# Adds moved to GpSimd, a channel norm over summed blocks, and one instruction block instead of two

## The chip, the cores and the metric

One core of one Trainium2 chip runs the kernel. The metric is the device time of one execution in microseconds (us). Five engines work from queues of their own: TensorE (PE; PEld is its weight load), VectorE (DVE), ScalarE (ACT), GpSimd (POOL) and SyncE (SP, which issues most of the DMAs). They wait for each other at semaphores.

## The reference

Two layers over a sequence of 1024 tokens of width 1024, all in fp32. What the change touches:

```python
# first block, its end
p_ssm = y_ssm @ w_branch_ssm;  p_att = y_att @ w_branch_att
merged = sigmoid(g_ssm) * p_ssm + sigmoid(g_att) * p_att
x = x + rmsnorm(merged @ w_out) * post_g
# second block
h = rms_norm(x);  proj = h @ w_in                        # conv (a, gate), q, k, v, two gates
y = causal_depthwise_conv(a * sigmoid(gate), width 31) + b   # 512 channels
conv = silu(layer_norm(y over the 512 channels))
attn = rms_norm(diff_attention(rms_norm(q), rms_norm(k), v))
merged = gate0 * (conv @ w_conv_out) + gate1 * (attn @ w_attn_out)
x = x + merged @ w_out
h2 = rms_norm(x)
x = x + mixture_of_experts(h2)                           # 32 experts, top 2 in one of 4 groups
```

## The kernel before

The kernel is a row of stages, each a set of programs for the five engines. Every large product keeps fp32 accuracy with three fp32r matmuls: high x high, high x low and low x high parts. ScalarE writes the high part (a rounded copy), VectorE the low part (the raw value less the high part).

`phase_dense` is the common loop. It takes a list of jobs, each a product with 512 output columns for the eight tiles of 128, whose results fill the eight PSUM banks. A step n is one k of one job: 24 matmuls of 512 columns. For each step ScalarE makes the high parts of the activations (L898) and of the weights (L880), VectorE the low parts (L945, L936), two steps ahead of TensorE at most. Behind the last k of a job the banks are evicted: by ScalarE (`act`, L922), or by VectorE as a multiply (`mul_T`, L972) or as a multiply and an add (`muladd_T`, L982 and L986, a pair for each bank, the second behind the first). TensorE starts a bank of the next job when its eviction is done. The last job walks the banks in the order 0, 2, 4, 6, 1, 3, 5, 7 (`HALVES`). Hooks let other work ride along in an engine's order: `aside(n)` on VectorE behind the low parts of step n, `beside(n)` on ScalarE behind the high parts, `middle[n]` on TensorE ahead of step n, `fill` on GpSimd, `fetch` on SyncE.

The stages in order: constants and the first norm; dense `xbc`; `phase_ssd`; then in one block the dense phase `bs`, the forgetting attention, dense `za` (its jobs 4 and 5, with eight steps each, are `muladd_T`), `phase_out_norm` and dense `q2` (2 x sigmoid and product, k, q, v). The block ends. `Chip.sem` registers a clear of each semaphore on GpSimd (L143), run when its stack is closed; `Chip.stage` closes it behind the block and then sets a barrier over all engines (L155). The next block holds `phase_diff_attention`, dense `gb2` and `phase_out_route`, and a third, with its own set of semaphores, the experts.

`gb2` has four gate jobs of eight steps (0 to 31), then two `mul_T` jobs with the attention output and two `muladd_T` jobs with the convolution's output, of four steps each (32 to 47). VectorE runs the convolution as taps (L741: source times a tap plus the accumulator, both in SBUF), two or three per step, in q2 and in gb2 up to step 31. `ChannelNorm` follows as hooks, counted from MEAN = 32: TensorE sums the four blocks of 128 channels with a matrix of ones ahead of step 32 (L2196, eight products of fp32 with 512 columns), ScalarE takes the mean (L2217), VectorE centres the blocks at steps 33 and 34 (L2239), ScalarE squares them at 34 and 35 (L2222), TensorE sums the squares ahead of step 36, VectorE adds eps at 37 (L2243), ScalarE takes the root at 38 (L2225), VectorE the reciprocal at 38 (L2247) and the products at 39 (L2251), ScalarE the Silus at 39 (L2230). Their result is the input of jobs 6 and 7, steps 40 on, which wait for it. The same hooks carry the split of the output weights (L3342 and L3355, one every second step).

The router ends with VectorE writing the slots of the tokens (L2461 to L2465) and GpSimd gathering the rows of the first two experts (L2509). The experts stage (`expert_programs`) loads each expert's three matrices of 2 MB, splits them (L2892 on ScalarE, L2957 on VectorE), turns the gathered rows (L2817), splits those (L2908, L2972), multiplies (L2808), and scatters with an add (L2782). A matrix's raw buffer is reloaded by SyncE as soon as its low parts are made. Gathers for later experts are L2765.

## Time and profile before

| | us |
|---|---|
| median of 3 runs (3044.0 to 3046.78) | 3046.55 |
| the profiled execution, its own time | 3043.43 |
| its span, first to last instruction | 3041.6 |
| mean granted TensorE clock | 0.961 |
| q2: last matmul starts / ScalarE's last eviction ends | 1792.53 / 1793.56 |
| gb2: last tap ends / low parts of step 35 end | 2129.98 / 2158.1 |
| gb2: TensorE starts steps 32, 36, 40, 44, 46 | 2143.97, 2174.75, 2206.70, 2230.50, 2249.84 |
| gb2: VectorE's evictions and low parts of step 37 end | 2171.19 |
| the router's first product starts | 2262.09 |
| VectorE writes the last slots | 2402.31 |
| the experts' first product starts / the last scatter is issued | 2421.69 / 3017.84 |

Times of the trace count from the start of the span. Engines overlap, so busy shares don't add up; idle time of an engine matters only where TensorE, or in the experts the transfers, wait for it. A row of a timeline gives the start, the duration (of all instructions merged in it), the engine, the line, and in brackets the idle time ahead of it with what ended that.

### The profile page before, as it was taken

The numbers are of one execution on the slowest core, as the hardware profiler recorded it, in microseconds if no ns is written. First come the engines' busy times: TensorE is split into PE (matmuls) and PEld (weight loads), VectorE is DVE, ScalarE is ACT, GpSimd is POOL, SyncE is SP. The second block draws the span as 40 slices with busy tenths as digits, with TensorE's granted clock in tenths as the row PEclk, the third lists the DMA queues.
The fourth block names the chain that finished last, engine by engine and source line by source line (L and its number), as shares of the span: only waits on it lengthen the run. The fifth ranks groups of instructions, "written<-read, shape, count | busy, mean of one in ns | idle before, by whom it ended". The sixth has DMA issues, their size and how long they took to land. (4 is left out here: it accounts for less than half of the span.)

```text
span 3041.6 us, 36124 instructions
## 1 busy us (share of the span) xinstructions
PE 2792.5 (92%) x13292; PEld 2281.5 (75%) x13302; DVE 1901.3 (63%) x2142; ACT 1440.0 (47%) x2105; POOL 482.1 (16%) x375
## 2 busy tenths in 40 slices
PE   6998999999989989999989987899899599999996
PEld 5787977888867666887878866778678488888874
DVE  3776745444345554435544876799563599888885
ACT  2544435323336655333333445533422277777773
POOL 0001400000006664000000000000000134434331
PEclk9999999999989999999999998999999699999998
DMA  3110011213466663121211100111212499999994
GB/s 93 42 49 15 1 57 42 101 46 104 159 187 132 139 131 77 49 104 42 91 56 51 49 15 1 29 46 46 89 53 116 172 364 384 369 366 368 363 356 150
DMA packets 159435, 387.95 MB, mean 128 GB/s; under 512 B 72769, under 2 KB 72897, under 8 KB 134720
## 3 DMA queue, kind: packets, MB, share of 16 engines
q1 hardware_dynamic: 150080, 369.27, 36.3%
q0 software_dynamic: 9216, 16.81, 2.2%
q8 instruction: 90, 1.47, 0.2%
q14 instruction: 49, 0.40, 0.0%
HBM read 347.93 MB, written 54.85 MB: 132 GB/s over the span
## 5 line engine op out<-in xcount | busy, mean ns | idle before, releaser
L2957 DVE TENSOR_TENSOR ex_w<-ex_raw,ex_w 128x2048 fp32r<-128x2048 f32 x190 | 430.8, 2289 | 77.5 <-ACT ex_w L2892 75.8
L2892 ACT ACTIVATE ex_w<-ex_raw 128x2048 fp32r<-128x2048 f32 x190 | 361.8, 1916 | 143.0 <-DMA ex_raw<-in_w_up_e 62.4
L2808 PE MATMUL ps<-ex_w,ex_xT 128*128 128x512 f32 x1536 | 368.3, 396 | 15.5 <-DVE ex_xT L2972 15.4
L2808 PEld LDWEIGHTS ps<-ex_w,ex_xT 128*128 128x128 f32 x1536 | 287.0, 190 | 82.0 <-issue 13.7
L945 DVE TENSOR_TENSOR bs_t<-arena,bs_t 128x1024 fp32r<-128x1024 f32 x88 | 107.7, 1224 | 270.0 <-ACT bs_t L898 269.9
L898 ACT ACTIVATE bs_t<-arena 128x1024 fp32r<-128x1024 f32 x88 | 93.3, 1061 | 294.6 <-PE ps L841 280.8
L741 DVE SCALAR_TENSOR_TENSOR arena<-arena,small 128x1023 f32<-128x1023 f32 (+9 forms) x168 | 213.5, 1271 | 3.6
L1276 POOL TENSOR_TENSOR fa_pl<-fa_p,fa_ph 128x512 fp32r<-128x512 f32 x192 | 191.9, 1015 | 103.5 <-ACT fa_ph L1397 100.8
L2808 PE MATMUL ps<-ex_w,ex_hT 128*128 128x512 f32 x768 | 182.9, 394 | 1.3 <-issue 1.1
L839 PE MATMUL ps<-bs_t,bs_w 128*128 128x512 f32 x448 | 175.3, 391 | 7.9 <-DVE bs_w L936 4.3
L840 PE MATMUL ps<-bs_t,bs_w 128*128 128x512 f32 x448 | 174.4, 389 | 0.0
L841 PE MATMUL ps<-bs_t,bs_w 128*128 128x512 f32 x448 | 174.3, 389 | 0.0
L839 PE MATMUL ps<-gb_t,gb_w 128*128 128x512 f32 x368 | 147.1, 400 | 20.9 <-DVE arena L972 7.0
L2808 PEld LDWEIGHTS ps<-ex_w,ex_hT 128*128 128x128 f32 x768 | 141.8, 188 | 31.6 <-issue 2.1
L1432 DVE TENSOR_REDUCE small<-ps 128x1 f32<-128x128 f32 (+7 forms) x128 | 96.7, 757 | 106.4 <-PE ps L1298 105.9
L839 PE MATMUL ps<-za_t,za_w 128*128 128x512 f32 x368 | 146.1, 397 | 8.9 <-DVE arena L986 4.1
L945 DVE TENSOR_TENSOR za_t<-arena,za_t 128x1024 fp32r<-128x1024 f32 x48 | 58.8, 1225 | 147.2 <-ACT za_t L898 147.1
L1387 ACT ACTIVATE fa_p<-ps 128x512 f32<-128x512 f32 x192 | 94.0, 490 | 108.6 <-PE ps L1330 66.1
L840 PE MATMUL ps<-gb_t,gb_w 128*128 128x512 f32 x368 | 145.1, 394 | 0.0
L840 PE MATMUL ps<-za_t,za_w 128*128 128x512 f32 x368 | 145.0, 394 | 0.0
L841 PE MATMUL ps<-gb_t,gb_w 128*128 128x512 f32 x368 | 145.0, 394 | 0.0
L841 PE MATMUL ps<-za_t,za_w 128*128 128x512 f32 x368 | 144.9, 394 | 0.0
(415 smaller groups left out, 6589.6 us busy)
## 6 DMA issues: line engine op xcount, KB each, us to landing
ex_raw<-in_w_gate_e SPq DMA_DIRECT2D x64, 1024.0 KB, 13.7
ex_raw<-in_w_up_e SPq DMA_DIRECT2D x64, 1024.0 KB, 13.1
ex_raw<-in_w_down_e SPq DMA_DIRECT2D x64, 1024.0 KB, 14.1
arena<-in_w_in SPq DMA_DIRECT2D x108, 512.0 KB, 3.5
arena<-in_x SPq DMA_DIRECT2D x4, 2048.0 KB, 11.1
arena<-in_w_out SPq DMA_DIRECT2D x16, 512.0 KB, 6.6
arena<-in_w_branch_ssm SPq DMA_DIRECT2D x8, 512.0 KB, 3.6
att_qh<-bs_split SPq DMA_DIRECT2D x2, 2048.0 KB, 8.8
```

What stands on the lines that cost most here:

```text
L741: ins = dve.scalar_tensor_tensor(out=acc[:, b, back:], in0=src[:, b, 0:SEQ - back], scalar=w, in1=acc[:, b, back:], op0=ALU.mult, op1=ALU.add)
L839: nc.tensor.matmul(c.ps[:, t, :], a[0], b[0], start=(k == 0), stop=False)
L840: nc.tensor.matmul(c.ps[:, t, :], a[0], b[1], start=False, stop=False)
L841: mm = nc.tensor.matmul(c.ps[:, t, :], a[1], b[0], start=False, stop=(n == last[j]))
L898: nc.scalar.activation(tp[s][0], jobs[j][0][:, k, :], ACT.Identity).then_inc(t_high, 1)
L945: V.tensor_tensor(tp[s][1], jobs[j][0][:, k, :], tp[s][0].bitcast(F32), ALU.subtract)\
L1276: nc.gpsimd.tensor_tensor(low[x % 4][:, 0:w], prob[x % 3][:, 0:w], f32(high[x % 4][:, 0:w]), ALU.subtract).then_inc(lowered, 1)
L1387: nc.scalar.activation(prob[x % 3][:, 0:w], c.ps[:, S_BANK[x % 3], 0:w], ACT.Exp)\
L1432: V.tensor_reduce(negmax[h % 2][:, t:t + 1], src, AX.X, ALU.max, negate=True)\
L2808: mm = nc.tensor.matmul(out, l, r, start=(k == 0 and n == 0), stop=(k == kc - 1 and n == 2))
L2892: nc.scalar.activation(half_of(part[m][0], h), raw[m][:, h * W // 2: (h + 1) * W // 2], ACT.Identity).then_inc(high[m], 1)
L2957: V.tensor_tensor(half_of(part[m][1], h), raw[m][:, h * W // 2: (h + 1) * W // 2], half_of(as_f32(part[m][0]), h), ALU.subtract)\
```

## The change

- `Chip.stage` sets no barrier behind its block. `Chip.retire` is new: GpSimd waits for some semaphores, closes a set (clears its semaphores) and signals `retired`. Dense `bs` to the experts now stand in one block with three sets: `first` (bs to out_norm), `second` (q2 and differential attention), `alive` (the rest). `first` is retired in q2, `second` in the last job of gb2. Differential attention waits for `retired[0]` and, engine by engine, for what the block's end stood for; the router waits for `retired[1]`.
- The experts' programs follow the router's in the same block. TensorE's first permissions to write the weights (`used`) move from the start of the experts to the router, behind "chosen".
- In `muladd_T` jobs but the last, VectorE only multiplies; GpSimd adds, bank by bank (semaphore `by_pool`). The merged product waits for all eight adds.
- `ChannelNorm`: GpSimd adds the four blocks and the four squared blocks (`on_pool`), TensorE sums one block over its channels. Root and reciprocal move from step 38 to 37, products and Silus from 39 to 38.

```diff
@@ -152,10 +152,20 @@
-        self.nc.all_engine_barrier()
-Dense = namedtuple("Dense", "product by_act by_vec kept w_low steps")
+    def retire(self, block, sems, waits, retired):
+        @block.gpsimd
+        def _(pool):
+            for s, n in waits:
+                pool.wait_ge(s, n)
+            sems.close()
+            pool.sem_inc(retired, 1)
...
@@ -812,6 +822,12 @@
         def _(pool):
+            for j, job in enumerate(jobs[:-1]):
+                if job[2] == "muladd_T":
+                    for t in range(TT):
+                        pool.wait_ge(by_vec, before(j, False) + t + 1)
+                        nc.gpsimd.tensor_tensor(job[3][:, t, :], job[4][:, t, :], job[3][:, t, :], ALU.add)\
+                            .then_inc(by_pool, 1)
         def _(pe):
...
@@ -978,6 +994,8 @@
+                    elif j < len(jobs) - 1:
+                        y = V.tensor_tensor(other[:, t, :], src, other[:, t, :], ALU.mult)
...
@@ -1534,6 +1552,7 @@
+            act.wait_ge(dense.by_pool, TT)
...
@@ -1919,10 +1938,15 @@
         def _(pe):
+            pe.wait_ge(retired, 1)
+            pe.wait_ge(normed, 2 * TT)
             def lay(x):
+                else:
+                    pe.wait_ge(dense.by_act, 3 * TT + x + 1)
...
@@ -1995,6 +2019,8 @@
         def _(act):
+            act.wait_ge(retired, 1)
+            act.wait_ge(dense.product, 5 * TT)
@@ -2032,6 +2058,9 @@
         def _(dve):
+            dve.wait_ge(retired, 1)
+            dve.wait_ge(dense.tapped, taps)
+            dve.wait_ge(lam.params, 16 * 8)
...
+    def on_pool(self, convolved):
+        pool, T = self.nc.gpsimd, self.nc.gpsimd.tensor_tensor
+        total = self.rstd
+        for b in range(1, self.NB):
+            convolved(pool, b)
+            if b > 1:
+                pool.wait_ge(self.by_blocks, b - 1)
+            T(total, total if b > 1 else self.av[:, 0, :], self.av[:, b, :], ALU.add)\
+                .then_inc(self.by_blocks, 1)
+        for b in range(1, self.NB):
+            pool.wait_ge(self.squared, b + 1)
+            if b > 1:
+                pool.wait_ge(self.by_blocks, self.NB + b - 2)
+            T(self.qv[:, 0, :], self.qv[:, 0, :], self.qv[:, b, :], ALU.add).then_inc(self.by_blocks, 1)
     def over_channels(self, src):
-        for b in range(self.NB):
-            for h in range(2):
-                mm = self.nc.tensor.matmul(c.ps[:, h, :], c.ones[:], src[:, b, h * BANK:(h + 1) * BANK],
-                                           start=(b == 0), stop=(b == self.NB - 1))
+        for h in range(2):
+            mm = self.nc.tensor.matmul(c.ps[:, h, :], c.ones[:], src[:, h * BANK:(h + 1) * BANK],
+                                       start=True, stop=True)
     def mean_on_tensor(self, pe, by_act, by_vec):
-        pe.wait_ge(self.convolved, 1)
-        self.over_channels(self.av).then_inc(self.meaned, 1)
+        pe.wait_ge(self.by_blocks, self.NB - 1)
...
+        self.over_channels(self.rstd).then_inc(self.meaned, 1)
     def variance_on_tensor(self, pe, by_act, by_vec):
-        pe.wait_ge(self.squared, self.NB)
-        self.over_channels(self.qv).then_inc(self.spread, 1)
+        pe.wait_ge(self.by_blocks, 2 * self.NB - 2)
+        self.over_channels(self.qv[:, 0, :]).then_inc(self.spread, 1)
     def on_scalar(self, n):
@@ -2220,10 +2264,10 @@
-        elif n == 6:
+        elif n == 5:
-        elif n == 7:
+        elif n == 6:
@@ -2242,10 +2286,9 @@
-        elif n == 6:
-        elif n == 7:
+        elif n == 6:
...
@@ -2382,6 +2425,7 @@
+            dve.wait_ge(retired, 1)
...
@@ -2597,6 +2644,8 @@
+            for used in experts_may:
+                pe.sem_inc(used, 1)
...
@@ -2877,8 +2926,9 @@
-        for m in range(3):
-            pe.sem_inc(used[m], 1)
+        if extra:
+            for m in range(3):
+                pe.sem_inc(used[m], 1)
...
@@ -3021,16 +3071,13 @@
-    return ExpertPrograms(sync, gpsimd, tensor, scalar, vector, half0, half1, stored)
-def phase_experts(c, x_dram, y_dram, experts, raw, loaded, gathered):
-    with ExitStack() as ctx:
-        main = expert_programs(c, ctx, "ex", x_dram, y_dram, experts, raw, loaded, gathered)
-        more = expert_programs(c, ctx, "xe", x_dram, y_dram, experts, expert_raw(c, True), main=main)
-        block = ctx.enter_context(c.nc.Block())
+    return ExpertPrograms(sync, gpsimd, tensor, scalar, vector, half0, half1, stored, used)
+def phase_experts(main, more, within):
+    with nullcontext(within) as (ctx, block):
...
-        with c.stage() as within:
-            differed = phase_diff_attention(c, q_tok, k_tok, lam, v2, o2, 4, 5, within)
+            c.retire(block, first, [(dense3.product, 2 * TT), (dense3.by_vec, TT), (dense3.w_low, 2 * KC + 1),
+                                    (out_normed.kept, 16 * TT)], retired[0])
+            differed = phase_diff_attention(c, q_tok, k_tok, lam, v2, o2, 4, 5, within, retired[0], dense3,
+                                            qk.normed, IN_Q2[-1])
+            ctx, within = alive, (alive, block)
...
@@ -3341,10 +3383,25 @@
+            def sum_blocks(pool, by_vec, kept):
+                def convolved(pool, b):
+                    if b == 3:
+                        pool.wait_ge(channels.convolved, 1)
+                    else:
+                        pool.wait_ge(blocks_done, b)
+                        pool.wait_ge(heads2.placed, TT)
+                channels.on_pool(convolved)
+            blocks_done = c.sem(ctx, "cn_blocks_done")
             def aside_gb2(n, tapped, by_act, by_vec, moved):
...
+                for b in range(3):
+                    if IN_GB2[n] < CW * (b + 1) - IN_Q2[-1] <= IN_GB2[n + 1]:
+                        nc.vector.wait_ge(tapped, IN_GB2[n + 1])
+                        nc.vector.sem_inc(blocks_done, 1)
                 if n == MEAN - 1:
...
+                        fill=sum_blocks,
+            c.retire(block, second, [(dense2.product, 2 * TT), (dense2.w_low, 2 * KC + 1)], retired[1])
+            main = expert_programs(c, ctx, "ex", xn, out[0], experts, raw, loaded, gathered)
+            more = expert_programs(c, ctx, "xe", xn, out[0], experts, expert_raw(c, True), main=main)
-                            within, parts2, dense2)
-            return c
-        phase_experts(c, xn, out[0], experts, raw, loaded, gathered)
+                            within, parts2, dense2, retired[1], main.used)
+            phase_experts(main, more, within)
...
```

## Rows read from the trace of the kernel before

**Rows 1.** The page, busy time of each engine.

```profile
PE 2792.5 (92%) x13292; PEld 2281.5 (75%) x13302; DVE 1901.3 (63%) x2142; ACT 1440.0 (47%) x2105; POOL 482.1 (16%) x375
```

**Rows 2.** Windows: stretch, its length, busy PE, PEld, DVE, ACT, POOL, clock, DMA share, GB/s.

```profile
2230.00:2250.00 20.00, 15.60 (x50) 11.31 (x50) 13.93 (x20) 4.11 (x5) 0.00 (x0) 0.74 0.00 1
2444.00:2990.00 546.00, 536.72 (x2507) 443.11 (x2506) 489.42 (x298) 407.84 (x296) 216.12 (x114) 1.00 1.00 368
```

**Rows 3.** GpSimd's semaphore clears at the two block ends: count, ns, first and last.

```profile
L143 POOLq EVENT_SEMAPHORE_RANGE_CLEAR  x90: 44/44/44, 1793.8 to 1800.4; - x90
...
L143 POOLq EVENT_SEMAPHORE_RANGE_CLEAR  x51: 44/44/44, 2410.0 to 2413.5; - x51
```

**Rows 4.** Timeline, TensorE and ScalarE behind the first of these.

```profile
1800.80 8.54 PE L1927 MATMUL ps<-ident,arena 128*128 128x128 f32 x64 [7.88 <-PEq L155]
...
1801.99 0.69 ACT L2002 ACTIVATE da_k<-ps,small 128x512 fp32r<-128x512 f32 x1 [8.43 <-PE ps L1927]
```

**Rows 5.** Timeline, TensorE around the gated jobs of za and gb2.

```profile
1413.72 0.47 PE L839 MATMUL ps<-za_t,za_w 128*128 128x512 f32 x1 [0.40 <-PE ps L841]
...
1464.31 0.39 PE L855 MATMUL ps<-za_t,za_w 128*128 128x512 f32 x1
...
2230.50 0.47 PE L839 MATMUL ps<-gb_t,gb_w 128*128 128x512 f32 x1 [0.30 <-PE ps L841]
...
2249.84 0.39 PE L853 MATMUL ps<-gb_t,gb_w 128*128 128x512 f32 x1
```

**Rows 6.** Timeline, VectorE's first multiply and last add of gb2's gated job.

```profile
2228.77 0.68 DVE L982 TENSOR_TENSOR arena<-ps,arena 128x512 f32<-128x512 f32 x1
...
2238.78 0.69 DVE L986 TENSOR_TENSOR arena<-arena 128x512 f32<-128x512 f32 x1
```

**Rows 7.** Timeline, TensorE: the two channel sums, the stalls of steps 39 and 40.

```profile
2135.75 7.10 PE L2196 MATMUL ps<-arena,ones 128*128 128x512 f32 x16 [0.30 <-PE ps L841]
...
2166.33 7.10 PE L2196 MATMUL ps<-arena,ones 128*128 128x512 f32 x16 [0.30 <-PE ps L841]
...
2193.97 0.50 PE L839 MATMUL ps<-gb_t,gb_w 128*128 128x512 f32 x1 [2.56 <-DVE gb_w L936]
...
2206.70 0.77 PE L839 MATMUL ps<-gb_t,gb_w 128*128 128x512 f32 x1 [6.99 <-DVE arena L972]
```

**Rows 8.** Timeline, VectorE and ScalarE: last taps, reciprocal, Silus.

```profile
2127.44 2.54 DVE L741 SCALAR_TENSOR_TENSOR arena<-arena,small 128x995 f32<-128x995 f32 x2
...
2184.55 6.55 DVE L2247 RECIPROCAL arena<-arena 128x1024 f32<-128x1024 f32 x1 [1.07 <-ACT arena L2225]
...
2196.42 4.64 ACT L2230 ACTIVATE arena<-arena,small 128x1024 f32<-128x1024 f32 x4
```

**Rows 9.** Timeline, start of the experts: gather's issue, turn of x, first product.

```profile
2402.95 1.22 POOL L2509 DMA_INDIRECT arena<-expert_in,ints  x1 [31.18 <-DVE ints L2461]
...
2414.65 1.94 PE L2817 MATMUL ps<-ident,arena 128*128 128x128 f32 x8 [13.25 <-DVEq L3018]
2421.69 2.93 PE L2808 MATMUL ps<-ex_w,ex_xT 128*128 128x512 f32 x6 [5.10 <-DVE ex_xT L2972]
```

**Rows 10.** Groups by line and shape: GpSimd's subtractions of 384 and 512 columns.

```profile
L1276 POOL TENSOR_TENSOR fa_pl<-fa_p,fa_ph 128x512 fp32r<-128x512 f32 x96 | 122.5, 1293 | 61.9 <-ACT fa_ph L1397 59.6 <-PE ps L1354 1.5
...
L1276 POOL TENSOR_TENSOR fa_pl<-fa_p,fa_ph 128x384 fp32r<-128x384 f32 x32 | 32.3, 1010 | 2.7 <-ACT fa_ph L1397 2.5
```

**Rows 11.** Timeline, a two-operand product of VectorE beside GpSimd's work and alone.

```profile
1164.96 2.26 DVE L1209 TENSOR_TENSOR arena<-arena,fa_rinv 128x1024 f32<-128x1024 f32 x1
...
1163.61 5.99 POOL L1276 TENSOR_TENSOR fa_pl<-fa_p,fa_ph 128x512 fp32r<-128x512 f32 x4 [0.96 <-ACT fa_ph L1397]
...
1190.51 1.21 DVE L1209 TENSOR_TENSOR arena<-arena,fa_rinv 128x1024 f32<-128x1024 f32 x1
```

**Rows 12.** Groups by line: indirect DMAs and VectorE's subtractions in the experts.

```profile
L2765 POOL DMA_INDIRECT arena<-expert_in,ints x30 | 73.9, 2465 | 27.5 <-POOL ints L2761 26.3 <-issue 1.2
...
L2957 DVE TENSOR_TENSOR ex_w<-ex_raw,ex_w 128x2048 fp32r<-128x2048 f32 x190 | 430.8, 2289 | 77.5 <-ACT ex_w L2892 75.8
```

102 lines of the change are left out of this document (49 added, 53 removed).

## The prediction

> **What bounds the kernel now.** I began with the page. TensorE is busy 92% of the span and no other engine over 63% [rows 1], so a microsecond counts only if TensorE loses it, except in the experts: there the DMA share is 1.00 at 368 GB/s over 546 us, TensorE 98% busy [rows 2]. Earlier stages are serial for TensorE; what they give back moves the experts' first transfer, and the end with it, one for one. Then I went along TensorE's timeline for its idle times. Five kinds lie where the change works: the two ends of a block (the clears of semaphores, then the first rows of TensorE and ScalarE behind them [rows 3, 4]); stalls behind VectorE's multiply-add pairs [rows 5, 6]; the two sums over channels [rows 7]; the stalls around the reciprocal [rows 7, 8]; the start of the experts [rows 9]. A matmul of 512 columns starts every 0.227 us at full clock (24 in a step of 5.44 us) and every 0.427 us at half; a step below is one k of a dense phase.
>
> **The profiled execution.** It took 3043.43 us; the median is 3046.55, 3.1 us (0.1%) more. I subtract from the former and carry the difference over.
>
> **1. End of the block before differential attention.** All engines are done by 1793.6. GpSimd then clears 90 semaphores from 1793.8 to 1800.4 [rows 3], 0.074 us each, and everybody waits: TensorE transposes at 1800.80, ScalarE splits at 1801.99 [rows 4]. After the change the clears are done during q2 (GpSimd's queue holds nothing else there), the first eight transposes follow the evictions bank by bank, and ScalarE's first split can start at about 1793.65. Gain 8.3 us. The new waits are for q2's v banks, the normed q and k and the last tap, all over by 1793.6. Bounds 7.8 to 8.9. The barrier after the xbc phase goes too; its clears (some 14 semaphores by the code) at 0.074 give 1.0 us, 0 to 1.3. The semaphores cleared at the very end change by two or so: nothing.
>
> **2. The adds of a gated job.** In za the step behind the first gated job starts at 1413.72, and the eight steps end at 1464.54; 192 matmuls at 0.227 are 43.5 us, so 7.3 are lost. In gb2 step 44 starts at 2230.50 and step 46 at 2249.84: 19.3 us instead of 10.9, 8.5 lost [rows 5]. The cause: VectorE works the pairs off from 2228.77 to 2239.4 at 1.33 us a bank, TensorE takes 0.68; and the granted clock over those 20 us is 0.74, so half of them pass at 1.2 GHz [rows 2, 6]. With the multiply alone VectorE needs 0.61 a bank; TensorE, which takes banks 0, 2, 4, 6 first, still waits some 0.5 for bank 6. GpSimd adds at 1.29 us for 128x512 [rows 10]: eight are 10.3 us, so it is still adding when VectorE turns to the low parts of the next step. That collides. A VectorE instruction that reads two SBUF operands, the product of L1209 with 1.21 us alone, takes 2.26 when GpSimd's adds stand beside it; GpSimd's next add ends late in turn, four spanning 5.99 us instead of 5.1 [rows 11]. I read: they take turns, a whole instruction each. So the two subtractions of the next step (1.22 and 0.68) each wait for one add and end at 2237.5, 1.1 us later than TensorE wants them at 2236.5. Lost after the change 0.5 + 1.1 = 1.6, and the half clock goes with the stalls. Gain 5.7 in za (3.5 to 6.8) and 6.8 in gb2 (4.0 to 7.9). ScalarE's new wait for all eight adds comes 20 us after them: hidden.
> The Trainium skill says the same against this change ("SBUF — State Buffer", Who interferes with whom): the read and write pair shared by VectorE and GpSimd is an exclusive lock. The row of L1209 agrees.
>
> **3. The mean.** Sixteen matmuls of fp32 take 7.10 us from 2135.75 [rows 7]; over one summed block there are four, 1.8. The third add needs the last tap (over at 2129.98 [rows 8]). A 128x1024 add is, from 1.01 us at 384 and 1.29 at 512 columns [rows 10], about 2.4: done at 2132.5, three before TensorE is there. Gain 5.3 (4.0 to 5.3). The two earlier adds land in the tap stretch, where VectorE runs about 2 us ahead of TensorE; each pushes it back 2.4. Cost 0.3, 0 to 3.
>
> **4. Variance, root, reciprocal.** The sum over squares also shrinks by 5.3 (7.10 from 2166.33 [rows 7]), but the low parts and evictions hold VectorE until 2171.2, so clean only 2.3 of it would count. Then VectorE waits for ScalarE's root (with its table load some 2.4 behind the variance) and runs the reciprocal (6.55 [rows 8]) a step earlier. The four products (4.6) and ScalarE's four Silus (4.64, and a table load [rows 8]) follow a step earlier too, before the high parts of step 39, so TensorE stalls there 4.5 us instead of 2.56; but the 6.99 before step 40 [rows 7] is gone, since the Silus are over. Worked through, step 40 starts at 2199.0 instead of 2206.70: 7.7. Against it stand GpSimd's three adds of squares, 7.1 us, among VectorE's two centrings, a w_low split and the low parts of step 35, all with two SBUF operands. By turns the low parts end at 2165.0 where TensorE wants them at 2160.3; the evictions and the variance move 3.6 behind. Left 4.1. The 4.5 us stall may bring the half clock, as the 6.99 did before; that evens out. Bounds 0 (both at once) and 9.5 (no turns, no slow stretch).
>
> **5. The experts.** Before, VectorE has the slots at 2402.3, GpSimd issues the gathers at 2402.95, and the block ends: its drain until 2409.8, then 51 clears to 2413.5 [rows 3]. TensorE turns x at 2414.65, the first product starts at 2421.69 [rows 9]. After the change ScalarE has split the first gate weights during the router, VectorE lowers them from 2402.4, and the chain is gather, turn (1.94), high (1.0), low (1.2), product: 4.35 us after the gather lands. If that landed at 2407.4, as it must have for the drain to end, the product starts at 2411.8, 9.9 sooner. But VectorE is now at its two-operand subtractions of 2.3 us [rows 12] while GpSimd writes the gather's descriptors: there an indirect DMA takes 2.47 us against 1.22 in the router [rows 9, 12], and its rows come later. With the landing of the later gathers (9.7 us behind the issue) the gain is 4.7. I take 7.0, in the middle, as both loads and products hang on it. SyncE's queue of weights moves by the same. TensorE's three increments now stand before the ranks, 0.15 each: cost 0.5.
> The Trainium skill differs here ("SBUF — State Buffer", SBUF: two separate sides): it names only a two-port op of VectorE as what starves descriptors, and lets an instruction with two inputs block only GpSimd ops that read SBUF. By it the gain would be 9.9, the time 3006 (a part of rival (a)); [rows 12] show the slow form beside such subtractions.
>
> **6. Retiring.** Clears of the second set (some 37) and the iotas now stand behind GpSimd's last add in its queue; all engines wait for them before the router. Adds end at 2241.3, 37 x 0.074 is 2.7, so 2244.5 against 2262: hidden by 17 us.
>
> **The sum.** 8.3 + 1.0 + 5.7 + 6.8 + 5.3 - 0.3 + 4.1 + 7.0 - 0.5 = 37.4. 3043.4 - 37.4 = 3006.0 on the profiled execution, 3009 on the median. The low ends of all terms add to 20.5 less, the high ends to 49 less: 3026 to 2997.5.
>
> **Rivals.** (a) The engines don't take turns and the gathers land as before: 5 and 4 are clean, 2 loses only 0.5. Then 37.4 + 2.2 + 3.6 + 2.9 = 46, so 3000. For it: GpSimd's own row in L1209's place shows one add unhindered. Chance 0.2. (b) GpSimd's adds win every turn, so that VectorE waits for the whole backlog, in 2 and in 4, and the tap stretch stalls: the whole 4 is lost, 2 gives 4 less, the taps cost 2.7 more: 26.5 left, so 3020. Against it: in L1209's place VectorE got in between two adds. Chance 0.18. (c) The block doesn't hide its clears, because GpSimd reaches them late (a wait in its queue I misread): 1 and 5 give nothing, 3024. Chance 0.04. (d) Slower than before: the longer stall in step 39 drops TensorE's clock and, with waits left by the turns, it stays at half until the router. Each matmul then costs 0.2 more; 8.5 steps of 24 are 41 us, against 37 gained: 3050. It decides from 185 matmuls at half clock on. Against it: the stretch of [rows 2] with 0.74 had some 10 us of it, and the last steps behind it ran at 0.227 again. Chance 0.03, a third of it for an end within 6 us of before. The forecast, 0.55.
>
> **Range and chances.** (a) and the better half of (b) must lie inside: 2997 to 3023. A difference of 0.2% (6 us) is about what a measurement of this kernel can tell from none: faster 0.97, same 0.01, slower 0.02.
>
> **What would show it.** No barrier rows and no gap over 1 us at either block end; step 40 of gb2 starts about 9 us after the sooner mean; VectorE's subtraction of step 35 at 2 to 3.5 us instead of 1.22; no half clock behind the gated jobs; the first expert product 9.5 us after the gathers' issue instead of 18.7. Wrong if the variance stretch gains over 7 (no turns) or nothing, or if the experts, bound by transfers, take clearly more than the 597 us that lie between their first product (2421.7) and the last scatter (3019).

## The result

The changed kernel takes 3002.02 us (median of 3001.13 to 3005.56) where the kernel before, with one more timing, takes 3045.28 (3040.06 to 3046.78): a ratio of 0.986, 95% interval 0.9842 to 0.9878, so 37 to 48 us less. The profiled execution took 3001.94 us against 3043.43, with a span of 3000.1. TensorE's busy time fell by 16.6 us against [rows 1], its idle time by 24.9.

```profile
PE 2775.9 (93%) x13278; PEld 2271.1 (76%) x13278; DVE 1912.2 (64%) x2126; ACT 1439.1 (48%) x2105; POOL 522.9 (17%) x397
```

Where the time went is read best by stage: the start of the first product of each stage on TensorE's timeline (a turn of rows ahead of it doesn't count), and the length from one to the next, in us. The last column is the range over the traces of the changed kernel and of all its variants below, without those that alter the stage.

| stage, from the first product of | before | changed | changed, second trace | gain | range |
|---|---|---|---|---|---|
| start of the span to xbc | 41.2 | 42.0 | 41.3 | -0.8 | 41.2 to 42.0 |
| xbc to bs | 346.7 | 349.7 | 345.4 | -3.0 | 341.3 to 349.8 |
| bs to forgetting attention | 501.9 | 501.3 | 501.7 | 0.6 | 501.1 to 501.9 |
| that to za | 300.8 | 299.8 | 297.4 | 1.0 | 295.4 to 299.8 |
| za to q2 | 380.3 | 374.3 | 374.2 | 6.0 | 373.4 to 374.7 |
| q2 to differential attention | 242.8 | 234.1 | 234.0 | 8.7 | 234.0 to 235.5 |
| that to gb2 | 137.4 | 136.0 | 138.8 | 1.4 | 135.9 to 139.9 |
| gb2 to its mean sum | 184.6 | 186.6 | 186.6 | -2.0 | 185.0 to 186.6 |
| mean sum to the router | 126.3 | 108.9 | 109.2 | 17.4 | 108.9 to 109.2 |
| router to the experts | 159.6 | 148.3 | 148.0 | 11.3 | 148.0 to 149.5 |
| experts to the end | 619.9 | 619.0 | 619.6 | 0.9 | 619.0 to 620.9 |

The four stages in which the change takes something away (za, q2, mean sum to router, router) give 43.4 together. The others lose 1.9 in this pair of traces; they are what makes the totals wander.

Differential attention, against [rows 3, 4]. Columns of the first row: count, ns, first and last start; the others are timelines of TensorE and ScalarE.

```profile
L143 POOLq EVENT_SEMAPHORE_RANGE_CLEAR  x111: 37/38/38, 1659.0 to 1666.4; - x111
```

```profile
1789.21 5.98 PE L1951 MATMUL ps<-ident,arena 128*128 128x128 f32 x53 [0.30 <-PE ps L857]
```

```profile
1789.96 0.69 ACT L2028 ACTIVATE da_k<-ps,small 128x512 fp32r<-128x512 f32 x1 [0.42 <-PE ps L1951]
```

GpSimd clears 111 semaphores from 1659.0 to 1666.4, in the middle of q2. TensorE's first transposes follow its last matmul (started at 1788.52) with 0.30 us between, where 7.88 stood, and ScalarE's first split comes 0.42 us behind its last eviction, where 8.43 stood.

The gated job of gb2, against [rows 5, 6] and the window in [rows 2]: GpSimd's eight adds, TensorE's last stall, and the window (length, busy PE, PEld, DVE, ACT, POOL, granted clock, DMA share, GB/s).

```profile
2207.09 12.89 POOL L829 TENSOR_TENSOR arena<-arena 128x512 f32<-128x512 f32 x8 [60.23 <-DVE arena L998]
```

```profile
2214.97 0.50 PE L855 MATMUL ps<-gb_t,gb_w 128*128 128x512 f32 x1 [0.62 <-DVE gb_w L952]
```

```profile
2206.00:2226.00 20.00, 18.84 (x81) 14.54 (x80) 18.55 (x19) 6.64 (x8) 13.27 (x11) 1.00 0.00 1
```

The adds take 1.61 us each, not 1.29, because they take turns with VectorE. TensorE's stalls of 0.23 and 0.62 are all that is left, and the granted clock is 1.00 instead of 0.74.

The channel norm, against [rows 7, 8]: TensorE's timeline (mean sum, step 35, step 36, step 39, step 40), then VectorE's low parts of step 35 and GpSimd's adds of squares.

```profile
2123.93 1.96 PE L2240 MATMUL ps<-arena,ones 128*128 128x512 f32 x4 [0.30 <-PE ps L857]
...
2147.46 0.80 PE L855 MATMUL ps<-gb_t,gb_w 128*128 128x512 f32 x1 [3.85 <-DVE gb_w L952]
...
2158.91 0.50 PE L855 MATMUL ps<-gb_t,gb_w 128*128 128x512 f32 x1 [1.98 <-DVE arena L2287]
...
2178.22 0.80 PE L855 MATMUL ps<-gb_t,gb_w 128*128 128x512 f32 x1 [2.68 <-DVE gb_w L952]
...
2185.71 0.47 PE L855 MATMUL ps<-gb_t,gb_w 128*128 128x512 f32 x1 [0.30 <-PE ps L857]
```

```profile
2141.23 3.43 DVE L961 TENSOR_TENSOR gb_t<-arena,gb_t 128x1024 fp32r<-128x1024 f32 x1
2144.58 2.83 DVE L952 TENSOR_TENSOR gb_w<-arena,gb_w 128x512 fp32r<-128x512 f32 x1
```

```profile
2136.33 2.76 POOL L2235 TENSOR_TENSOR arena<-arena 128x1024 f32<-128x1024 f32 x1 [15.63 <-ACT arena L2266]
2140.82 6.04 POOL L2235 TENSOR_TENSOR arena<-arena 128x1024 f32<-128x1024 f32 x2 [1.73 <-ACT arena L2266]
```

Each sum is 1.96 us instead of 7.10. The price stands at step 35: VectorE's subtractions of 1024 and 512 columns take 3.43 and 2.83 us (1.22 and 0.68 alone), 2.21 and 2.15 longer, about one add of GpSimd each (2.40 where nothing holds it up); TensorE stalls 3.85 us ahead of step 35 and works at half clock for 3.1 us behind it (a matmul every 0.427 us). The stall of 6.99 before step 40 is gone.

The start of the experts, against [rows 9]: GpSimd's two gathers, VectorE's first subtractions, TensorE's turn of x and first product.

```profile
2372.23 1.22 POOL L2554 DMA_INDIRECT arena<-expert_in,ints  x1 [29.74 <-DVE ints L2505]
2373.76 1.91 POOL L2554 DMA_INDIRECT arena<-expert_in,ints  x1 [0.30 <-issue]
```

```profile
2372.49 4.49 DVE L3007 TENSOR_TENSOR ex_w<-ex_raw,ex_w 128x2048 fp32r<-128x2048 f32 x2 [0.90 <-DVE small L2509]
```

```profile
2376.77 1.98 PE L2866 MATMUL ps<-ident,arena 128*128 128x128 f32 x8 [6.10 <-DMA arena<-expert_in,ints]
2381.12 13.53 PE L2857 MATMUL ps<-ex_w,ex_xT 128*128 128x512 f32 x48 [2.37 <-DVE ex_xT L3022]
```

The turn starts 4.54 us behind the first gather's issue and the first product 8.89 behind it, instead of 18.74.

### The profile page after: what moved, and what is told of

Read it like the earlier page. It is cut to its first block, busy times and chain, and to the rows that moved or that the text cites. A ratio compares the mean times of both kernels' runs of the same rounds, so it can differ in the third digit from the quotient of the medians.

```text
span 3000.1 us, 36062 instructions
## 1 busy us (share of the span) xinstructions
PE 2775.9 (93%) x13278; PEld 2271.1 (76%) x13278; DVE 1912.2 (64%) x2126; ACT 1439.1 (48%) x2105; POOL 522.9 (17%) x397
## 4 chain that ended last, share of the span: by engine, by line
PE 51%; DMA 12%; DVE 10%; issue 5%; ACT 4%; POOL 4%; SPq 0%; POOLq 0%; DVEq 0%; ACTq 0%; PEldq 0%
PE ps L855 12%; PE ps L857 12%; PE ps L856 12%; DMA ex_raw<-in_w_up_e 6%; DMA ex_raw<-in_w_down_e 5%; POOL fa_pl L1294 4%; DVE ex_w L3007 3%; PE ps L2857 3%; ACT ex_w L2942 2%; PE ps L2605 1%; PE ps L1663 1%; PE ps L2607 1%; PE ps L1665 1%; PE ps L2606 1%; PE ps L1664 1%
## 5 line engine op out<-in xcount | busy, mean ns | idle before, releaser
L1405 ACT ACTIVATE fa_p<-ps 128x512 f32<-128x512 f32 x192 | 93.8, 489 | 107.6 <-PE ps L1348 75.7
```

Of the source, the lines that this page charges most:

```text
L1405: nc.scalar.activation(prob[x % 3][:, 0:w], c.ps[:, S_BANK[x % 3], 0:w], ACT.Exp)\
```

## The experiments

Each kernel below is the changed one with one part undone or altered. The medians carry the wandering stages of the table, so each is read by its stage as well. Medians of kernels that ran together can be compared with each other, but the intervals of most neighbours overlap; each group is set against the kernel before on its own chip (3044.4 us for the first four, 3041.93 for the next four, 3042.43 for the last four).

| kernel | median, us | against before, 95% interval | stage that it touches, us | same stage, changed |
|---|---|---|---|---|
| squares on VectorE | 2998.66 | 0.985 (0.9832 to 0.9867) | mean sum to router 107.6 | 108.9 |
| squares on TensorE | 3001.38 | 0.9855 (0.9836 to 0.9873) | the same 108.0 | 108.9 |
| norm late | 3007.25 | 0.988 (0.9859 to 0.9901) | the same 116.1 | 108.9 |
| gated adds on VectorE | 3011.26 | 0.9892 (0.9872 to 0.9911) | za 380.4, mean sum to router 114.4 | 374.3, 108.9 |
| experts in an own block | 3005.85 | 0.9881 (0.9854 to 0.9907) | router 159.1, experts 616.7 | 148.3, 619.0 |
| late clears | 3009.6 | 0.989 (0.9863 to 0.9918) | q2 243.9 | 234.1 |
| late split | 2999.05 | 0.9853 (0.9826 to 0.9881) | router 151.2, experts 620.1 | 148.3, 619.0 |
| fills for the squares | one time, 3001.21 | | mean sum to router 107.6 | 108.9 |
| changed kernel again | 2999.27 | 0.9847 (0.9823 to 0.9872) | the same 109.2 | 108.9 |
| mean on TensorE | 3009.09 | 0.9872 (0.9843 to 0.9902) | the same 115.5 | 109.2 |
| banks of the sum last | 2993.18 | 0.9834 (0.9807 to 0.9862) | the same 104.3 | 109.2 |
| the same, norm a step later | 2996.54 | 0.9841 (0.9818 to 0.9864) | the same 103.7 | 109.2 |

### What do the turns with GpSimd cost?

The theory is that of the prediction: VectorE's instructions with two SBUF operands and GpSimd's adds take turns, and this is the stall at step 35. Three variants move the adds of squares.

Squares on VectorE:

```diff
 def on_pool(self, convolved):
-        for b in range(1, self.NB):
-            pool.wait_ge(self.squared, b + 1)
...
-            T(self.qv[:, 0, :], self.qv[:, 0, :], self.qv[:, b, :], ALU.add).then_inc(self.by_blocks, 1)
 def on_vector(self, n):
+        if n in (2, 3):
+            for b in ((1,), (2, 3))[n - 2]:
+                V.wait_ge(self.squared, b + 1)
+                V.wait_ge(self.by_blocks, self.NB + b - 2)
+                V.tensor_tensor(self.qv[:, 0, :], self.qv[:, 0, :], self.qv[:, b, :], ALU.add)\
+                    .then_inc(self.by_blocks, 1)
```

> The changed kernel, with the three adds of squares on VectorE (the first at step 34, two at step 35) instead of GpSimd. Theory (turns): the 3.85 us stall ahead of step 35 and the half clock behind it come only from VectorE's two-operand instructions waiting for GpSimd's adds (3.43, 3.43, 2.83 us instead of 1.21, 1.21, 0.68). Three adds of 1.13 on VectorE itself fit: low parts of step 35 done 1.7 us before TensorE asks. Step 36 then starts 3.3 us sooner (about 2155.6 against 2158.91), the kernel 3 us faster than the changed one: 2999. Rival 1 (the evictions or the eps step bind anyway): step 36 within 0.5 us of where it is, 3002. Rival 2 (VectorE has no room): low parts of step 36 come late, 3 us slower, 3005.

Timelines of VectorE (low parts of step 35) and TensorE (variance sum, step 36) of this kernel:

```profile
2136.70 1.22 DVE L961 TENSOR_TENSOR gb_t<-arena,gb_t 128x1024 fp32r<-128x1024 f32 x1
2137.84 0.68 DVE L952 TENSOR_TENSOR gb_w<-arena,gb_w 128x512 fp32r<-128x512 f32 x1
```

```profile
2145.91 1.95 PE L2235 MATMUL ps<-arena,ones 128*128 128x512 f32 x4 [0.30 <-PE ps L857]
2151.97 0.80 PE L855 MATMUL ps<-gb_t,gb_w 128*128 128x512 f32 x1 [4.11 <-DVE arena L2288]
```

The subtractions are back at 1.22 and 0.68 and there is no stall at step 35. From step 32 to step 36 it takes 28.4 us instead of 31.9 (2151.97 less 2123.55, against 2158.91 less 2127.00): 3.5 where 3.3 were expected. But 2.2 of them are lost again by the router: VectorE runs its evictions and the low parts of step 37 first and comes to eps at 2150.70, so TensorE now waits 4.11 us in one piece and works at half clock from 2151.97 to 2157.3. The stage is 1.3 us shorter; the two ratios to the kernel before have intervals that overlap, so the total doesn't show it.

Squares on TensorE:

```diff
 def variance_on_tensor(self, pe, by_act, by_vec):
-        pe.wait_ge(self.by_blocks, 2 * self.NB - 2)
-        self.over_channels(self.qv[:, 0, :]).then_inc(self.spread, 1)
+        pe.wait_ge(self.squared, self.NB)
+        for b in range(self.NB):
+            for h in range(2):
+                mm = self.nc.tensor.matmul(self.c.ps[:, h, :], self.c.ones[:],
+                                           self.qv[:, b, h * BANK:(h + 1) * BANK],
+                                           start=(b == 0), stop=(b == self.NB - 1))
+        mm.then_inc(self.spread, 1)
```

> The changed kernel, with the squares of the four blocks summed on TensorE as before (16 matmuls, 7.1 us), GpSimd summing only the blocks of the mean. Theory (turns): the stall of step 35 (3.85) and its half clock (1.2) go, the longer sum costs 5.1 but stands beside VectorE's evictions and low parts; step 36 starts 1.5 us sooner than in the changed kernel, 3000.5. Rival (GpSimd's adds cost VectorE little and the shorter sum is what was gained): step 36 starts 2.3 to 5 us later, 3004 to 3007.

Timeline of TensorE of this kernel:

```profile
2148.24 7.10 PE L2250 MATMUL ps<-arena,ones 128*128 128x512 f32 x16 [0.30 <-PE ps L857]
2156.66 0.50 PE L855 MATMUL ps<-gb_t,gb_w 128*128 128x512 f32 x1 [1.32 <-DVE arena L2287]
```

Step 36 starts 30.8 us behind step 32 (2125.87), 1.1 sooner than in the changed kernel, where 1.5 were expected; the stage is 1.0 shorter. The three adds of squares on GpSimd thus gave nothing: what they took from TensorE, 5.1 us, went to the turns and more.

Fills for the squares: GpSimd only writes where it added, so this kernel leaves out the sum of squares.

```diff
-            T(self.qv[:, 0, :], self.qv[:, 0, :], self.qv[:, b, :], ALU.add).then_inc(self.by_blocks, 1)
+            pool.memset(self.qv[:, b, :], 1.0)
+            pool.memset(self.qv[:, 0, :], 1.0).then_inc(self.by_blocks, 1)
```

> The changed kernel, with each of GpSimd's three adds of squares replaced by two fills of 128x1024 (0.92 us each in the router's rows), which write and do not read; the sum of squares is left out, so the variance is wrong. Theory (turns are taken over reads of two SBUF operands): VectorE's centring and low parts keep 1.21, 1.21 and 0.68 us, no stall ahead of step 35. Rival (any instruction of GpSimd holds VectorE's two-operand instructions off): they wait up to 0.9 us each, low parts of step 35 come 1 to 2 us late. Time: as with the squares on VectorE or better, 2998.

Timelines of GpSimd (the first pair of fills) and VectorE (two centrings):

```profile
2135.33 0.95 POOL L2235 MEMSET arena<- 128x1024 f32 x1 [15.61 <-ACT arena L2267]
2136.22 0.95 POOL L2236 MEMSET arena<- 128x1024 f32 x1
```

```profile
2134.63 2.35 DVE L2284 TENSOR_TENSOR arena<-arena 128x1024 f32<-128x1024 f32 x2
```

Two centrings with two SBUF operands each take 2.35 us together while a fill runs beside them, where the changed kernel needed 4.56 beside one add, and the split behind them keeps its 1.22 beside the second fill. The low parts of step 35 have 1.23 and 0.68, but a fill stands beside them only in their last 0.3 us. The engines take turns over reads, not over being busy at once. The Trainium skill ("SBUF — State Buffer", Who interferes with whom) says the same: an instruction with two SBUF inputs contends with a GpSimd instruction that reads SBUF, not with one that only writes it. The traces agree.

### Root and reciprocal a step sooner

```diff
 def on_scalar(self, n):
-        elif n == 5:
+        elif n == 6:
             act.wait_ge(self.step, 1)
...
-        elif n == 6:
+        elif n == 7:
             act.wait_ge(self.params, 32)
...
 def on_vector(self, n):
+        elif n == 6:
             V.wait_ge(self.rooted, 1)
             V.reciprocal(self.rstd, self.rstd).then_inc(self.step, 1)
-        elif n == 6:
+        elif n == 7:
             V.wait_ge(self.step, 2)
```

> The changed kernel, with root and reciprocal back at step 38, products and Silus back at step 39. Theory: steps 36 to 40 took 31.95 us before and 26.8 after, so the move alone is worth 5.2: TensorE stalls 2.6 at step 39 and 7 at step 40, half clock behind it, and the kernel takes 3007. Rival (the gain there came from the sums, since the Silus only moved their stall from step 40 to step 39): within 1.5 us of the changed kernel, 3002 to 3003.5.

Timeline of TensorE, steps 39 and 40 of this kernel:

```profile
2175.06 0.80 PE L855 MATMUL ps<-gb_t,gb_w 128*128 128x512 f32 x1 [2.56 <-DVE gb_w L952]
...
2187.79 0.77 PE L855 MATMUL ps<-gb_t,gb_w 128*128 128x512 f32 x1 [5.46 <-DVE arena L988]
```

From step 36 to the router it takes 81.04 us instead of 73.95. Step 40 comes 5.1 us later, as the theory had it, with a stall of 5.46, and the half clock behind it costs 2.0 more. Undoing the move costs 7.1 us, more than the mean's shorter sum gave (5.1).

### The gated adds

```diff
-                        pool.wait_ge(by_vec, before(j, False) + t + 1)
-                        nc.gpsimd.tensor_tensor(job[3][:, t, :], job[4][:, t, :], job[3][:, t, :], ALU.add)\
-                            .then_inc(by_pool, 1)
...
-                    elif j < len(jobs) - 1:
-                        y = V.tensor_tensor(other[:, t, :], src, other[:, t, :], ALU.mult)
```

> The changed kernel, with the adds of the gated jobs back on VectorE, behind each multiply. Theory (VectorE's pair of 1.33 us against TensorE's 0.68 a bank is the whole loss): za loses 5.9 and gb2 7.1 again, 13.0 together, 3015. Rival (part of the gain came from the half clock that follows a stall only sometimes): half of each is stall, half clock, so between 7 and 9 slower, 3009 to 3011, with a granted clock near 1 over the job.

Window of gb2's gated job (columns as above):

```profile
2208.00:2228.00 20.00, 15.54 (x56) 11.27 (x55) 15.51 (x22) 4.11 (x5) 0.00 (x0) 0.83 0.00 1
```

za is 6.1 us longer and the stage of gb2 5.4, so 11.5 together; the clock is 0.83 where [rows 2] had 0.74. The theory's 13.0 was too much and the rival's 7 to 9 too little. The pairs cost their stall each time; of the half clock behind it, more or less comes (in gb2 12 matmuls at half clock in the kernel before, 6 here). The median, 3011.26, shows some 2 us less than the stages.

### The block ends

Late clears:

```diff
-                                    (out_normed.kept, 16 * TT)], retired[0])
+                                    (out_normed.kept, 16 * TT), (dense3.by_act, 4 * TT)], retired[0])
```

> The changed kernel, with GpSimd's clears of the first set of semaphores held until ScalarE has made q2's last eviction; the block still doesn't end. Theory (the time lay in the 90 clears, 6.6 us, and not in the barrier): TensorE's first transposes wait for the clears, the kernel is 7.2 to 8 us slower than the changed one, about 3010. Rival (the barrier of all engines was the cost, and differential attention's start hides clears): 0 to 3 us slower, 3002 to 3005.

The clears (columns as above) and TensorE's first transposes:

```profile
L143 POOLq EVENT_SEMAPHORE_RANGE_CLEAR  x111: 37/38/38, 1785.5 to 1792.9; - x111
```

```profile
1792.97 7.29 PE L1951 MATMUL ps<-ident,arena 128*128 128x128 f32 x51 [8.21 <-POOLq L143]
```

With no barrier at all the stage takes 243.9 us, as long as the one before (242.8). The time lay in the clears, 111 of them in 7.4 us. Of the 9.7 us over the changed kernel 7.9 are TensorE's wait (8.21 less 0.30), 0.8 come behind it, up to the first product, and 1.0 lies in q2 ahead of its last matmul, which the edit doesn't touch; the same stage differs by 1.5 among the other traces.

Experts in a block of their own (a barrier and a block behind the router, the experts' semaphores in it, `used` set at its start):

```diff
+        nc.all_engine_barrier()
+        with ExitStack() as ctx:
+            main = expert_programs(c, ctx, "ex", xn, out[0], experts, raw, loaded, gathered)
+            more = expert_programs(c, ctx, "xe", xn, out[0], experts, expert_raw(c, True), main=main)
+            block = ctx.enter_context(nc.Block())
+            phase_experts(main, more, (ctx, block))
```

> The changed kernel, with the experts again in a block of their own: behind the router the semaphores are cleared, all engines meet at a barrier, then the experts begin. Theory (the block's end and the splits behind it held the first product back, and the gathers are not slowed by VectorE's subtractions): the first product starts 18.7 us behind the gather's issue again instead of 8.9, and with the first reload of weights it moves all that follows, so the end comes 10 to 11.5 us later: 3012 to 3014. Rival (the experts are bound by transfers, which catch up): under 5 us, 3007 or less.

The clears, and TensorE's first product:

```profile
L143 POOLq EVENT_SEMAPHORE_RANGE_CLEAR  x75: 37/38/38, 2369.5 to 2374.6; - x75
```

```profile
2382.80 13.22 PE L2857 MATMUL ps<-ex_w,ex_xT 128*128 128x512 f32 x48 [5.10 <-DVE ex_xT L3021]
```

The first product starts 20.0 us behind the gather's issue (2362.85) and the stage is 10.9 us longer. The experts' stage is 2.4 shorter (616.7 against 619.0, and all others are at 619.0 or more), but the transfers don't make anything up: from the first product to the last scatter's issue it takes 598.2 us, where the changed kernel has 595.2 and the other variants 595.3 to 597.1. What is shorter is the end, since the 75 clears of the router's end don't stand there. The clears behind the last scatter, of the changed kernel and of this one:

```profile
L143 POOLq EVENT_SEMAPHORE_RANGE_CLEAR  x156: 37/38/47, 2989.8 to 3000.1; - x156
```

```profile
L143 POOLq EVENT_SEMAPHORE_RANGE_CLEAR  x81: 37/38/47, 2994.3 to 2999.4; - x81
```

From the last scatter's issue to the end of the span it is 18.5 us instead of 23.8. So 8.5 us are left in the trace, between the two theories, but the rival's reason is wrong: the late start comes through to the last scatter in full, as the theory had it, and 5.3 us come back because clears were moved off the end. The medians show less, 3005.85 against 3002.02; the ratios to the kernel before (0.9881 and 0.986, with intervals that overlap) put it at 6.

Late split:

```diff
             if after:
+                if after is FIRST:
+                    act.wait_ge(gathered[0], 16)
                 hi(GATE)(*after)
```

> The changed kernel, with ScalarE's split of the first gate weights held until the first gather has landed, as late as a block of its own would make it. Theory (the splits done ahead are a part of the gain, the clears and the drain the rest): ScalarE needs 3.7 us behind the landing, VectorE two subtractions of 2.3; the first product starts 3.3 us later (12.2 behind the gather's issue) and so does the first reload of weights, later still (6 to 8 us) but with its raw buffers full, so the end comes 3 to 7 us later: 3005 to 3009. Rival (transfers catch up, or the landing of rows alone binds): within 1 us of the changed kernel, 3001 to 3003.

Timelines of GpSimd (the count and the gather of the next expert) and of TensorE's first product:

```profile
2375.80 2.22 POOL L2810 COPY ints<-ints 128x1 int32<-128x1 int32 x1 [3.73 <-PE ps L2866]
2378.88 2.19 POOL L2814 DMA_INDIRECT arena<-expert_in,ints  x1 [0.86 <-POOL ints L2810]
```

```profile
2381.37 9.00 PE L2857 MATMUL ps<-ex_w,ex_xT 128*128 128x512 f32 x27 [5.63 <-DVE ex_xT L3024]
```

The first product starts 11.85 us behind the gather's issue (2369.52), 3.0 later than in the changed kernel; the experts' 620.1 is within their range, so the cost is 3 us by the stages, at the low edge of the theory. The median (2999.05) does not show it; it is below that of the changed kernel, so by totals alone the rival would stand. Of the 11.3 us at the start of the experts some 3 come from the splits made during the router, 1.5 were gained ahead of the gather's issue, and the other 6.9 come from the clears, GpSimd's drain and the barrier. In passing it shows the cost that the prediction feared: GpSimd's copy takes 2.22 us and its indirect DMA 2.19 (0.18 and 1.02 in the changed kernel at this place) where VectorE's subtractions stand beside them. The copy ends 0.04 us behind the subtraction that it began beside (2378.02 and 2377.98), the indirect DMA 0.9 behind (2381.08 and 2380.18).

### How far do totals wander?

> The changed kernel once more, unaltered, beside the three that follow. In nine traces the stretch from the first xbc product to the first bs product took 341.3 to 349.8 us with the same code, so its total should lie within 4 us of 3002; the stretches the change touches should repeat within 1 us: za 374.3, q2 to differential attention 234.1, gb2 295.5, router to experts 148.3.

The changed kernel again gave 2999.27, and its touched stages 374.2, 234.0, 295.8 (gb2 whole) and 148.0, as expected. Its xbc to bs took 345.4. Windows over 16 us that begin 21 to 26 us behind xbc's last product, of the changed kernel, its second trace, and the one with the experts in their own block:

```profile
296.00:312.00 16.00, 14.75 (x71) 13.80 (x70) 7.61 (x9) 6.72 (x21) 4.20 (x3) 0.54 0.00 1
```

```profile
296.00:312.00 16.00, 15.39 (x84) 14.83 (x85) 6.45 (x9) 7.21 (x27) 2.44 (x2) 0.68 0.00 1
```

```profile
296.00:312.00 16.00, 15.39 (x118) 14.56 (x118) 8.78 (x12) 9.13 (x33) 5.62 (x3) 1.00 0.00 1
```

The same code has a granted clock of 0.54, 0.68 or 1.00 here, and 71, 84 or 118 matmuls in 16 us. A second such place lies at 96 to 104 us (0.59 in the changed kernel, 1.00 in the other two). Where both are slow the stretch from xbc to bs takes 349.3 to 349.8 us, where neither is, 341.3 to 341.6: the range of 8.5 us. A third, smaller one stands at step 8 of gb2 (185.0 or 186.6 up to the mean sum): TensorE waits 2.47 us ahead of step 8 in the changed kernel and with the experts in their own block alike, and works at half clock for 3.4 us behind it in the first and not at all in the second.

### The mean, and a faster kernel

Mean on TensorE:

```diff
 def mean_on_tensor(self, pe, by_act, by_vec):
-        pe.wait_ge(self.by_blocks, self.NB - 1)
-        self.over_channels(self.rstd).then_inc(self.meaned, 1)
+        pe.wait_ge(self.convolved, 1)
+        for b in range(self.NB):
+            for h in range(2):
+                mm = self.nc.tensor.matmul(self.c.ps[:, h, :], self.c.ones[:],
...
+        mm.then_inc(self.meaned, 1)
```

> The changed kernel, with the mean's four blocks summed on TensorE as before (16 matmuls). Theory (the 5.1 us of shorter sum stand wholly on TensorE's path, GpSimd's adds among the taps cost nothing): gb2 takes 5.1 us more, 300.6, the kernel 3007. Rival (the adds among the taps push VectorE back, or the later mean lets the turns of step 34 and 35 fall elsewhere): gb2 2 to 4 us more.

```profile
2125.12 7.10 PE L2242 MATMUL ps<-arena,ones 128*128 128x512 f32 x16 [0.30 <-PE ps L857]
```

The row is TensorE's mean sum again. GpSimd's three adds of the mean are left out here. The stage is 6.4 us longer than in the changed kernel beside it: 5.1 in the sum and 1.2 more from step 32 to 36, where the half clock behind the stall of step 35 lasts longer (2153.8 to 2159.9). gb2 up to its sum takes 186.3 without the adds among the taps and 186.6 with them. As a whole it takes 301.8 where the theory had 300.6, so the adds among the taps cost next to nothing, as it said.

Banks of the sum last: the squares on VectorE, and TensorE takes the two banks that hold the channel sum at the end of steps 32 and 36.

```diff
-                if middle is not None and n in middle:
-                    middle[n](pe, by_act, by_vec)
+                late = middle[n](pe, by_act, by_vec) if middle is not None and n in middle else None
...
-                for t in walk(j):
+                for t in (2, 3, 4, 5, 6, 7, 0, 1) if late else walk(j):
+                    if late and t == 0:
+                        late()
...
 def variance_on_tensor(self, pe, by_act, by_vec):
-        pe.wait_ge(self.step, 1)
+        return lambda: pe.wait_ge(self.step, 1)
```

> The kernel with the squares added on VectorE, and TensorE taking banks 2 to 7 first in steps 32 and 36, the two banks that hold the channel sum last, so that it waits for the mean and for eps only there. Theory: TensorE's wait of 4.1 us between variance and step 36 and the half clock behind it go, 6.3 us sooner at the end of step 36; but the reciprocal (6.55) then holds the low parts of step 38 (2.6 us) and the Silus the high parts of step 39 (4.7), so that only 1.8 us are left and, with the mean's 1.1, gb2 takes 291.3 against 294.2 there: 2996. Rival (VectorE's chain from eps on doesn't bind): 6 us or more, 2991.

Timeline of TensorE, steps 38 and 39 of this kernel:

```profile
2150.88 0.50 PE L856 MATMUL ps<-gb_t,gb_w 128*128 128x512 f32 x1 [2.26 <-DVE gb_w L953]
...
2160.84 0.50 PE L856 MATMUL ps<-gb_t,gb_w 128*128 128x512 f32 x1 [2.58 <-DVE gb_w L953]
```

The stage is 104.3 us, 3.3 shorter than with the squares on VectorE alone, where 2.9 were expected, and 4.9 shorter than in the changed kernel beside it. The stalls came at the places foreseen (2.26 for the low parts of step 38, behind the reciprocal, where 2.6 were expected, and 2.58 at step 39, where 4.7 were), and half clock stands behind both. With 2993.18 us its median is the lowest here, 6.1 us below the changed kernel beside it; the intervals of the two overlap, and 4.9 is what the stage shows.

The same with products and Silus behind the parts of step 39:

```diff
 def on_scalar(self, n):
-        elif n == 6:
+        elif n == 7:
             act.wait_ge(self.params, 32)
...
 def on_vector(self, n):
-        elif n == 6:
+        elif n == 7:
             V.wait_ge(self.step, 2)
```

> As the one before, and with the four products and the Silus a step later, behind the low and high parts of step 39 (root and reciprocal stay at step 37). Theory: TensorE stalls 2.6 us at step 38 behind the reciprocal, not at step 39, and about 1 at step 40; step 40 starts 7.6 us sooner than with the squares on VectorE alone, gb2 takes 285.5 to 287, the kernel 2990 to 2992. Rival (the Silus late by a step hold step 40, as they did in the kernel before): step 40 stalls 4 us or more with half clock behind it, gb2 about 292, 2996.

Timelines of TensorE (steps 38 and 40) and of VectorE (the last w_low split and the evictions of job 5):

```profile
2156.90 0.51 PE L856 MATMUL ps<-gb_t,gb_w 128*128 128x512 f32 x1 [2.22 <-DVE gb_w L953]
...
2172.50 0.76 PE L856 MATMUL ps<-gb_t,gb_w 128*128 128x512 f32 x1 [4.39 <-DVE arena L989]
```

```profile
2170.54 1.22 DVE L3414 TENSOR_TENSOR w_low<-arena,w_high 128x1024 fp32r<-128x1024 f32 x1
2171.67 4.87 DVE L989 TENSOR_TENSOR arena<-ps,arena 128x512 f32<-128x512 f32 x8
```

gb2 takes 290.3 us as a whole, where 285.5 to 287 were expected: the rival had it. Step 39 doesn't stall, but step 40 does, 4.39 us. My sum ended with its low parts at 2170.5 and left out what stands behind them on VectorE: a split of 1.22 us and the evictions of job 5, for which step 40 waits bank by bank. The stage is still 0.5 us shorter than with the banks alone, while the median is 3.4 us higher; the intervals overlap, so which of the two is faster stays open.

## Why the prediction was right, and where it was off

The forecast was 3009 us with 37.4 gained; measured were 3002.02 and 43.4 in the four stages (41.5 between the two profiled executions). By its steps:

1. End of the block before differential attention: 8.3 forecast, 8.7 in the stage. Right, and by its own reason, as the late clears show. The 1.0 for xbc's barrier can't be told in a stage that ranges over 8.5.
2. Gated adds: 5.7 and 6.8 forecast. za gave 6.0. In gb2 the lead over the kernel before grew from 22.4 us (at step 44) to 29.3 (at step 46), so 6.9. The turns were there (GpSimd's adds at 1.61 us, VectorE's next two subtractions at 2.11 and 1.77), and the half clock went with the stalls.
3. The mean: 5.3 forecast; from the sum's start to step 32 it is 3.07 us instead of 8.22, so 5.15. For the taps 0.3 was set, and 0.3 is what the mean on TensorE wins there; the rest of the 2.0 lost ahead of the sum is the half clock at step 8 of gb2, which comes and goes.
4. Variance, root and reciprocal: 4.1 forecast, 5.4 measured (a lead of 17.0 us at step 32, 22.4 at step 41). The turns cost what was worked out: the low parts of step 35 were forecast 4.7 late and TensorE's start moved by 4.0; step 36 was to lose 1.3 us of lead (3.6 less 2.3) and lost 1.1. From there on 5.4 were forecast and 6.6 measured. The term that was off is the stall at step 39, forecast at 4.5 us and measured at 2.68. Of this 1.3 is a table load (rows below): the sum put it between eps and the root, but ScalarE ran it ahead, while VectorE was still at its low parts, and the root started 0.03 us behind eps (2158.86). The other 0.5 stays open. The half clock did even out, as the forecast said: it costs 1.5 us behind step 39, and the 1.5 behind step 40 in the kernel before is gone. Step 40 itself comes 26.8 us behind step 36, where the forecast had 26.55, but by a shorter stall and a slower clock than it counted.
5. The experts: 7.0 forecast with 4.7 and 9.9 as bounds, less 0.5; the stage gave 11.3. This is the term that was mis-sized, by 4.8 of the 6.0 us that the forecast was off. The chain from turn to first product (4.35) was right to the hundredth; wrong was that the gathers would land later beside VectorE's subtractions. The first was issued 0.26 us ahead of the first subtraction (2372.23 and 2372.49) and kept its 1.22; only the second, which the first product doesn't need, took 1.91 and ended 0.9 us behind the subtraction beside it. The slow form exists, as the late split shows; it missed the one transfer that matters. This gives 9.85 us instead of 7.0, so 2.9 of the 4.8. TensorE's increments, set at 0.5, cost nothing: the lead was 29.2 at the router's start and 29.6 at the ranks. Another 1.1 came between the ranks and the gather's issue, where the forecast had nothing: TensorE's 32 matmuls behind its wait of 9.41 us take 5.77 us instead of 6.84. In the other traces of the same code they take 5.58 to 6.69, so a part of it is luck.
6. Retiring the second set: hidden, as forecast.

ScalarE's timeline for step 4, the table load and the root:

```profile
2156.40 1.28 ACT L2269 ACT_TABLE_LOAD   x1
2158.89 1.06 ACT L2269 ACTIVATE arena<-arena 128x1024 f32<-128x1024 f32 x1 [1.21 <-DVE arena L2287]
```

Of the rivals, (a) gave 3000 with no turns and prompt gathers. Its number is closer than the forecast's, but its reason is half true: the gathers were prompt, the turns were there, and where it had the sums clean it took in 3.6 us that didn't come. (b), GpSimd winning every turn, didn't come: each VectorE instruction waited for one add at most. (c) and (d) didn't come. The rule of the Trainium skill ("SBUF — State Buffer", SBUF: two separate sides) weighed in step 5 gave 9.9 us for the gathers, and 9.85 was measured (18.74 less 8.89). The number is right by the order of issue and doesn't bear the rule out: the rows of the late split don't fit it, with 2.19 us for an indirect DMA beside subtractions of two operands and 1.02 without, nor does the second gather here. An indirect DMA reads its list of rows from SBUF, which may be what waits; that wasn't tried.

## What to carry to other kernels

Work moved to GpSimd is not free where VectorE reads two SBUF operands in the same microseconds: here three adds saved TensorE 5.1 us and cost 4.0 in stall and 1.6 in half clock, while the same adds on VectorE itself, in its idle time, brought no stall there. Ahead of a merge of stages, look at the number of semaphores that are cleared between them; at the first block end here the clears were the price, not the barrier. Those at the very end count as well: 155 before and 156 after the change take the last 10.3 us of the span, and the change leaves them there. And where totals wander by more than the effect, read the stage: the medians would have hidden the 3 us of the late split, which the rows of its stage show.

## What was not expected

- The semaphores of a set are cleared while GpSimd's engine still works: in the changed kernel the 37 clears of the second set stand at 2211.3 to 2213.6 and its adds run from 2207.09 to 2219.98. The queue runs ahead of the engine.
- A single wait of 4.1 us ahead of step 36 brought 5.3 us of half clock; waits of 1.3 (in the kernel before) and 1.98 (in the changed one) brought none at the same place. What becomes of the clock behind a stall of 2 to 3 us differs: behind step 39's stall of 2.68 half clock lasted 3.1 us in the changed kernel; behind 2.09 with the squares on VectorE it came 1.3 us late and lasted 3.4; behind 2.56 it lasted 3.1 with the norm late, and behind the same 2.56 in the kernel before there was none. Why was not tried.
